# Encoder trunk step on one core: activation tiles as two rows of 144 columns, even and odd tokens, read by TensorE in pairs

## The reference

```
x = x + 0.5 * swiglu_ffn(x)          # D_MODEL 2048, D_FF 5504, float32
h = rmsnorm(x); z = h @ w_in         # columns for three attention groups
o = concat(A, B, C)                  # A: index top-k attention, B: window, C: chunk band
x = x + o @ w_out
x = x + 0.5 * swiglu_ffn(x)
swiglu_ffn: (silu(h @ w_gate) * (h @ w_up)) @ w_down
```

## Time and profile before

| | |
|---|---|
| median of 3 timed runs | 2038.17 us (2037.7 to 2039.73) |
| profiled execution, span from first to last instruction | 2037.9 us |
| mean granted TensorE clock | 0.999 of full speed |
| PE busy | 2030.6 us, 100% |
| DVE busy | 1170.2 us, 57% |
| ACT busy | 846.5 us, 42% |
| transfers | 339.96 MB, mean 167 GB/s |

### The profile page before, as it was taken

One profiled execution on the slowest core, in us unless ns is written; L12 is line 12 of the kernel. 1 busy time (PEld: TensorE's weight loads), 2 busy tenths in 40 slices (PEclk: granted clock), 3 DMA queues, 4 the chain that ended last, 5 costly groups with the idle time before them and its releaser, 6 DMA issues.

```text
span 2037.9 us, 41985 instructions
## 1 busy us (share of the span) xinstructions
PE 2030.6 (100%) x15805; PEld 2010.8 (99%) x15805; DVE 1170.2 (57%) x1790; ACT 846.5 (42%) x1290; POOL 88.5 (4%) x140
## 2 busy tenths in 40 slices
PE   9999999999999999999999999999999999999999
PEld 8999999999999999999999999999999999999999
DVE  7555445555455566588889765555445555455544
ACT  6333333333333344345668644333333333333332
POOL 0000000000000000022432000000000000000000
PEclk9999999999999999999999999999999999999999
DMA  7554555545545545544453454555544555555554
GB/s 256 167 169 161 174 162 170 173 167 163 172 163 169 171 157 180 181 143 159 153 154 110 151 165 165 166 169 173 173 163 165 167 168 172 172 165 166 168 184 146
DMA packets 101274, 339.96 MB, mean 167 GB/s; under 512 B 12149, under 2 KB 16293, under 8 KB 101200
## 3 DMA queue, kind: packets, MB, share of 16 engines
q1 hardware_dynamic: 95856, 329.41, 49.8%
q0 software_dynamic: 2960, 7.45, 1.3%
q10 hardware_dynamic: 2400, 2.33, 0.3%
HBM read 334.45 MB, written 5.28 MB: 167 GB/s over the span
## 4 chain that ended last, share of the span: by engine, by line
PE 97%; DVE 1%; ACT 1%; issue 0%; DMA 0%; SPq 0%; DVEq 0%; ACTq 0%
PE bank L601 31%; PE bank L602 31%; PE bank L603 31%; PE bank L688 1%; PE bank L721 1%; PE bank L703 1%; PE bank L665 0%; DVE w_lo L1367 0%; DMA raw<-in_w_ffn_up 0%; PE bank L903 0%; ACT w_hi L1056 0%; ACT s_buf L1113 0%; PE bank L705 0%; DVE z_prep L1448 0%; ACT z_prep L1113 0%
## 5 line engine op out<-in xcount | busy, mean ns | idle before, releaser
L601 PE MATMUL bank<-h_hi_and_lo,w_hi 128*128 128x288 f32 x3344 | 985.8, 295 | 1.9 <-DVE w_lo L1624 1.5
L602 PE MATMUL bank<-h_hi_and_lo,w_hi 128*128 128x288 f32 x3344 | 981.7, 294 | 0.0
L603 PE MATMUL bank<-h_hi_and_lo,w_lo 128*128 128x288 f32 x3344 | 981.5, 294 | 0.0
L1367 DVE TENSOR_TENSOR w_lo<-raw,w_hi 128x1024 fp32r<-128x1024 f32 x634 | 729.8, 1191 | 199.1 <-ACT w_hi L1056 198.7
L1056 ACT ACTIVATE w_hi<-raw 128x1024 fp32r<-128x1024 f32 x634 | 617.4, 1021 | 316.3 <-PE bank L603 314.0
L601 PEld LDWEIGHTS bank<-h_hi_and_lo,w_hi 128*128 128x128 f32 x3344 | 630.6, 189 | 6.5 <-DVE w_lo L1624 2.9
L602 PEld LDWEIGHTS bank<-h_hi_and_lo,w_hi 128*128 128x128 f32 x3344 | 630.7, 189 | 0.2
L603 PEld LDWEIGHTS bank<-h_hi_and_lo,w_lo 128*128 128x128 f32 x3344 | 630.7, 189 | 0.0
L602 PE MATMUL bank<-gu_hi_and_lo,w_hi 128*128 128x288 f32 x1376 | 403.6, 293 | 0.0
L603 PE MATMUL bank<-gu_hi_and_lo,w_lo 128*128 128x288 f32 x1376 | 403.6, 293 | 0.0
L601 PE MATMUL bank<-gu_hi_and_lo,w_hi 128*128 128x288 f32 x1376 | 403.6, 293 | 0.0
(11 more groups left out here) (205 smaller groups left out, 986.5 us busy)
## 6 DMA issues: line engine op xcount, KB each, us to landing
raw<-in_w_ffn_gate SPq DMA_DIRECT2D x168, 512.0 KB, 4.5
raw<-in_w_ffn_up SPq DMA_DIRECT2D x168, 512.0 KB, 4.5
raw<-in_w_ffn_down SPq DMA_DIRECT2D x96, 512.0 KB, 3.8
raw<-in_w_in SPq DMA_DIRECT2D x74, 512.0 KB, 4.7
raw<-in_w_ffn_down SPq DMA_DIRECT2D x64, 384.0 KB, 4.2
raw<-in_w_out SPq DMA_DIRECT2D x32, 512.0 KB, 4.5
raw<-in_w_ffn_down SPq DMA_DIRECT2D x32, 448.0 KB, 4.4
bias_rev<-bias_vectors POOLq DMA_DIRECT2D x11, 256.0 KB, 5.0
```

The source lines that it names most:

```text
L601: pe.matmul(out, w_hi[b][:, k, :], hi, start=(k == first_k), stop=False)
L602: pe.matmul(out, w_hi[b][:, k, :], lo, start=False, stop=False)
L603: mm = pe.matmul(out, w_lo[b][:, k, :], hi, start=False, stop=(k == last_k))
L1367: dve.tensor_tensor(w_lo[b][:, k, :], raw_tile(ph, j, s)[:, k, :], w_hi[b][:, k, :].bitcast(F32), ALU.subtract)\
```

## The change

The three kinds of split tiles get another layout, and PE another reading order. A tile still takes 320 words. It is now two rows of 144 columns, the second 160 words after the first, and without the 24 words ahead. The first row has the even tokens and the second the odd tokens. PE streams column 0 of the first row, column 0 of the second, column 1 of the first, and so on; that is tokens 0, 1, 2, 3, and the bank is written front to back. ACT and DVE write the two rows from a source that they read at every second column. The extra words at the end of the rooms go, and `key_hi` and `key_lo` start at the tile's first word.

The instructions of every engine stay in the same order, and on PE, POOL and SP each row is the same; on ACT and DVE the instructions that write split tiles change their shape from 4 times 72 to 2 times 144 columns, and DVE has a few register instructions less.

```diff
-            spread = room[:, PAD:PAD + 2 * tiles * TILE].rearrange("p (t a b) -> p t a b", a=NT // BLOCK, b=APART)[:, :, :, 0:BLOCK]
+            spread = room[:, 0:2 * tiles * TILE].rearrange("p (t s i) -> p t s i", s=2, i=APART)[:, :, :, 0:NT // 2]
             return spread[:, 0:tiles], spread[:, tiles:2 * tiles], room
-        def blocks(row):
-            return row.rearrange("p (a b) -> p a b", b=BLOCK)
-        BLOCK, APART, TILE, PAD = 72, 80, 320, 24
-        h_hi, h_lo, _ = right_sides("h_hi_and_lo", DT, tail=64)
+        def two_rows(row):
+            return row.rearrange("p (i s) -> p s i", s=2)
+        def in_pairs(two):
+            return two.rearrange("p s i -> p i s")
+        APART = 160
+        TILE = 2 * APART
+        h_hi, h_lo, _ = right_sides("h_hi_and_lo", DT)
...
-            gu_hi, gu_lo, gu_room = right_sides("gu_hi_and_lo", thirds[0], ffn_scope, tail=PAD)
-        o_hi, o_lo, o_room = right_sides("o_hi_and_lo", 16, tail=PAD)
+            gu_hi, gu_lo, gu_room = right_sides("gu_hi_and_lo", thirds[0], ffn_scope)
+        o_hi, o_lo, o_room = right_sides("o_hi_and_lo", 16)
...
-        key_hi, key_lo = (o_room[:, t * TILE + PAD:t * TILE + PAD + NT] for t in (5, 16 + 5))
+        key_hi, key_lo = (o_room[:, t * TILE:t * TILE + NT] for t in (5, 16 + 5))
...
-                    hi, lo = (t[:, ::-1, ::-1] for t in rhs(k))
+                    hi, lo = (in_pairs(t) for t in rhs(k))
                     b = buf(ph, s)
-                    out = blocks((bank or bank_w[b])[:, 0:NT])[:, ::-1, ::-1]
+                    out = (bank or bank_w[b])[:, 0:NT].rearrange("p (i s) -> p i s", s=2)
                     pe.matmul(out, w_hi[b][:, k, :], hi, start=(k == first_k), stop=False)
                     pe.matmul(out, w_hi[b][:, k, :], lo, start=False, stop=False)
                     mm = pe.matmul(out, w_lo[b][:, k, :], hi, start=False, stop=(k == last_k))
...
-                act.activation(h_hi[:, j, :, :], blocks(xT[:, j, :]), ACT.Copy, scale=g_cols[:, bass.ds(j + index * DT, 1)]).then_inc(hhi_rdy, 1)
+                act.activation(h_hi[:, j, :, :], two_rows(xT[:, j, :]), ACT.Copy, scale=g_cols[:, bass.ds(j + index * DT, 1)]).then_inc(hhi_rdy, 1)
```

More of the change, by code:

```diff
@@ L1135, in out_hi @@
                 act.wait_ge(pv_done, U + (3 * p + 3))
-                act.activation(o_hi[:, tile, :, :], blocks(bank_o[:, 0:NT]), ACT.Copy).then_inc(ohi_rdy, 1)
+                act.activation(o_hi[:, tile, :, :], two_rows(bank_o[:, 0:NT]), ACT.Copy).then_inc(ohi_rdy, 1)
             def prep_items(step):
@@ L1272, in body @@
                         act.wait_ge(gu_rdy, F + 1)
-                        act.activation(gu_hi[:, j, :, :], blocks(gu[:, :]), ACT.Copy).then_inc(guh_rdy, 1)
+                        act.activation(gu_hi[:, j, :, :], two_rows(gu[:, :]), ACT.Copy).then_inc(guh_rdy, 1)
                     bodies(act, ph, body, peel_first=3 if ph.n0 == 0 else ph.more["first"])
@@ L1375, in h_tile @@
                 dve.wait_ge(hhi_rdy, H + 1)
-                dve.scalar_tensor_tensor(h_lo[:, j, :, :], blocks(xT[:, j, :]), g_cols[:, bass.ds(j + index * DT, 1)],
+                dve.scalar_tensor_tensor(h_lo[:, j, :, :], two_rows(xT[:, j, :]), g_cols[:, bass.ds(j + index * DT, 1)],
                                          h_hi[:, j, :, :].bitcast(F32), ALU.mult, ALU.subtract).then_inc(hlo_rdy, 1)
@@ L1488, in out_lo @@
                 dve.wait_ge(ohi_rdy, body * 2 + (p + 1))
-                dve.tensor_tensor(o_lo[:, tile, :, :], blocks(bank_o[:, 0:NT]), o_hi[:, tile, :, :].bitcast(F32), ALU.subtract).then_inc(olo_rdy, 1)
+                dve.tensor_tensor(o_lo[:, tile, :, :], two_rows(bank_o[:, 0:NT]), o_hi[:, tile, :, :].bitcast(F32), ALU.subtract).then_inc(olo_rdy, 1)
             def attention_pairs(body, splits, reads, tiles, sums, late):
@@ L1615, in lower @@
                     dve.wait_ge(hhi_rdy, t + 1)
-                    dve.scalar_tensor_tensor(h_lo[:, t, :, :], blocks(xT[:, t, :]), g_cols[:, t:t + 1], h_hi[:, t, :, :].bitcast(F32),
+                    dve.scalar_tensor_tensor(h_lo[:, t, :, :], two_rows(xT[:, t, :]), g_cols[:, t:t + 1], h_hi[:, t, :, :].bitcast(F32),
                                              ALU.mult, ALU.subtract).then_inc(hlo_rdy, 1)
@@ L1691, in body @@
                         dve.wait_ge(guh_rdy, F + 1)
-                        dve.tensor_tensor(gu_lo[:, j, :, :], blocks(gu[:, :]), gu_hi[:, j, :, :].bitcast(F32), ALU.subtract).then_inc(gul_rdy, 1)
+                        dve.tensor_tensor(gu_lo[:, j, :, :], two_rows(gu[:, :]), gu_hi[:, j, :, :].bitcast(F32), ALU.subtract).then_inc(gul_rdy, 1)
                     bodies(dve, ph, body, peel_first=3 if ph.n0 == 0 else ph.more["first"])
```

## The result

The changed kernel takes 1934.43 us (median of 4 runs, 1931.46 to 1935.31) against 2038.33 us: a ratio of 0.949 (95% interval 0.947 to 0.950), 5.1% faster. Forecast were 2002 us and a gain of 1.8%. The direction was right, the size was not: 104 us in place of 37.

A forecast was written before the change was run, and what follows sets the result against it. The prediction took PE's stream of matmuls, 130 ns from start to start, as the bound. From 2037.9 us, -37.3 for the stream and +0.7 for writing tiles gave 2001.3 profiled, about 2002 timed; range 1920 to 2105 us.

The forecast's parts named there:

- What bounds the kernel: Whole kernel: one stream of 14,928 matmuls on PE, 130.0 ns from start to start, 1940.6 us or 95% of the span.
- The pool of 10 ns: Each matmul: 130 ns against 120 scaled from 240 at half clock; 149 us at the very most to be had.
- The mechanism: PE's moving read: clashes with the next weights' load cost time; two half-speed rows could avoid them.
- The value within the bounds: Matmul start distance, bounded by 120 and 240 ns: a quarter of the loss goes, 127.5 ns, -37.3 us.
- Rival A: All matmuls: the loss is a fixed cost each, so column order does nothing; 2039 us, chance 0.20.
- Rival C: All matmuls: pairs end the weight clash altogether, 120 to 123 ns, 1889 to 1934 us; chance 0.08.
- Rival B: Moving read of all matmuls: jumps cost rate; in part 130.3 to 136 ns, chance 0.14; in full 3680 us, 0.20.
- Writers: ACT and DVE split-tile writes: every-second-column reading adds 0.12 and 0.15 us each, nearly all hidden; 0.7 us counted.
- What a faster stream meets: Other engines and DMA: at 127.5 ns per matmul they have room to spare, so nothing else becomes late.
- Theory L: PE's column reads, proposed during follow-ups: two readers alternate columns, each at full speed only taking all 4 words per 16-byte line.

The follow-up runs named there:

- every second word: The changed kernel with each tile one contiguous row, of which PE reads first all even words, then all odd words: 3926.03 us.
- step 4: The changed kernel with each tile one contiguous row, read as two rows 144 words apart in pairs, taking every fourth word: 3968.11 us.

## Why the prediction was right in sign and wrong in size

- *What bounds the kernel*: held. PE's stream, counted from start to start, carried the whole of the gain.
- *The pool of 10 ns*: 7.5 of it could be had. The slow-clock rows gave the size of the pool rightly, and what is left at 122.5 ns is 2.5 ns over 120. That the data side doesn't follow the granted clock, which I only guessed from them, the run with every second word bears out (257 ns at either level). The Trainium skill ("TensorE: Matmul & The Clock Gate", Back-to-back issue gap) gives columns at 2.4 GHz plus about 2.5 ns for isolated matmuls, and another spacing for a stream with weight loads. The stream after, with a load for each matmul, agrees with the first to 0.1 ns.
- *The mechanism*: the step "a clash of the moving stream with the next weights" failed. Halved weight loads moved the mean distance by 0.6 ns of the 9. In its place the runs show the 16-byte lines: the loss follows how many words of a line are taken before the next (122.5 ns with 4, 128.8 to 133.3 with 2), and 2 words of offset alone turn 122.5 into 133.3.
- *The value within the bounds*: this is the term that was mis-sized, 2.5 ns taken and 7.5 measured, -37.3 us against -112.0. I chose a quarter because two contiguous matmuls in the earlier trace rows started 130 ns apart as the blocks did. That only said that a row is as bad as blocks. It said nothing on pairs, and I used it as if it did.
- *Rival A (a fixed cost)*: its evidence, one distance in all three rooms, was true of any cause that depends on the order within a tile alone, as here. *Rival C* came true in its size (its end at 123 ns and 1934 us), though not by its clash with the weights: I gave it 0.08.
- *Rival B (jumps cost)*: false for jumps between two lines that are each used up. For jumps that are not it is true with more than its full price of 240 ns: 259.7 in the run with step 4. The Trainium skill's rule ("SBUF — State Buffer", Specifications: at least two hits on a 16-byte line) was the reason against the change. Read as two hits by consecutive columns it is refuted both ways: pairs have none and are fastest, every second word has two and takes 256.5 ns. Counted for each of two alternating readers it sorts the runs, but two hits still cost 6 to 11 ns here; only four are free.
- *Writers*: ACT 29 ns more where I took 120, DVE none where I took 150. The first up phase gave 0.8 us less than its due, near the 0.7 that I had put down for the writers, but they are not its cause. The 1187th product starts at 166.34 us before and 158.22 after; with rows 144 apart and with pairs 24 words in, whose writers read every second word too, it starts at 157.42 and 157.51. That is 8.9 and 8.8 us earlier than before, where 8.9 were due. What the changed kernel loses there stays open; its repeat has 158.13.
- *What a faster stream meets*: "nothing else becomes late" failed in the attention stage: 3.6 us went there beside the clock's 3.4, and with rows 144 apart, at full clock, 3.4 us.

## What to carry to other kernels

Read the distance of matmul starts against the columns at the granted clock: of 130 ns against 120, 7.5 could be had, 5% of the kernel, while PE showed 100% busy. When 4-byte columns are streamed at the full clock, lay them so that even and odd columns each walk through whole 16-byte lines, with both rows starting on such a line; one word order does it, even with rows 4 words apart, and an offset of 2 words undoes it. This was measured for fp32r and 288 columns alone. And a bound far from both ends should not be filled in by the nearest row if that row doesn't vary the thing that changes.

## What was not expected of the hardware

- The same 288 words cost 122.5 to 259.7 ns by order alone (1931 to 3968 us for the kernel).
- Streaming blocks backwards is 3.2 ns per matmul faster than forwards (130.0 and 133.2). No theory here explains it.
- Four rows in turn (153.3 ns) beat runs of two from two rows (186.5 ns), though in both a reader takes one word per visit. Theory L would need a reader that keeps more than one line; that was not tested.
